# One block per layer: the second norm and the odd input projection taken into the feed-forward block, front reordered

## What is computed

```
def trunk(x, ...):
    for i in range(2):
        if i == 0: y = even_mixer(x, ...)   # latent attention and a gated short convolution -> w_o_e
        else:      y = odd_mixer(x, ...)    # x @ w_in_o, conv of 4 taps, silu, gated delta rule -> w_o_o
        x = layer_norm(ALPHA * x + y, ln_mix_g[i], ln_mix_b[i])
        h = x @ w_ff_in                     # 1024 -> 2 * 2816: gate, up
        gate = conv3(h[..., :2816])         # per channel, 3 taps
        y = (silu(gate) * up) @ w_ff_out    # 2816 -> 1024
        x = layer_norm(ALPHA * x + y, ln_ff_g[i], ln_ff_b[i])
def odd_mixer(x, ...):
    qkv, z, a, bt = split(x @ w_in_o)       # 3072, 1024, 8, 8 columns
    qkv = silu(conv4(qkv)); beta = sigmoid(bt)
    g = -exp(a_log) * softplus(a + dt_bias) # summed inside chunks of 64 tokens: G
    ...                                     # delta rule over 17 chunks and 8 heads, rms norm, * silu(z), @ w_o_o
```

## Time and profile before

| | us |
|---|---|
| runs of the kernel before | 3303.55, 3304.77, 3307.37 |
| the profiled execution, its own time | 3306.29 |
| its span, first to last instruction | 3304.5 |
| PE matmul busy | 3082.5 (93%), 22758 matmuls |
| PE weight loads busy | 2930.9 (89%) |
| DVE busy | 1582.0 (48%) |
| POOL busy | 1062.7 (32%) |
| ACT busy | 722.6 (22%) |
| mean granted clock of TensorE, as a share of 2.4 GHz | 0.966 |

### The profile page before, as it was taken

The page is one execution under the profiler, slowest core; times in us unless marked ns, Lnnn a source line. Parts: engine busy times, 40 slices in busy tenths (PEclk is TensorE's granted clock), DMA queues, the critical chain, the costliest instruction groups (busy, mean ns, idle before and its releaser), DMA issues. The chain is left out here.

```text
span 3304.5 us, 54021 instructions
## 1 busy us (share of the span) xinstructions
PE 3082.5 (93%) x22758; PEld 2930.9 (89%) x22758; DVE 1582.0 (48%) x2701; ACT 722.6 (22%) x1346; POOL 1062.7 (32%) x708
## 2 busy tenths in 40 slices
PE   7998999999999999985999949998899999999996
PEld 6997668899999999965999948887889999999994
DVE  2337574654443443453666645554364344434444
ACT  2112473210100111121121234553131001001102
POOL 2233101243233232204323246774443332232220
PEclk8999999999999999997999979998899999999998
DMA  5120102011111111103322233331401111111101
GB/s 160 44 62 7 45 1 81 13 52 45 39 42 56 44 45 39 33 1 107 99 85 86 79 80 85 82 89 40 125 21 50 50 53 39 45 41 43 39 26 55
DMA packets 261885, 184.23 MB, mean 56 GB/s; under 512 B 49775, under 2 KB 246749, under 8 KB 261541
## 3 DMA queue, kind: packets, MB, share of 16 engines
q1 hardware_dynamic: 261669, 181.09, 18.8%
HBM read 147.19 MB, written 33.84 MB: 55 GB/s over the span
## 5 line engine op out<-in xcount | busy, mean ns | idle before, releaser
L145 PE MATMUL ps<-xhi,whi 128*128 128x364 f32 (+1 forms) x3528 | 1171.1, 332 | 67.6 <-POOL wlo L138 41.9
L146 PE MATMUL ps<-xlo,whi 128*128 128x364 f32 (+1 forms) x3528 | 1166.3, 331 | 0.0
L151 PE MATMUL ps<-xhi,wlo 128*128 128x364 f32 (+1 forms) x3528 | 1165.3, 330 | 0.0
L145 PEld LDWEIGHTS ps<-xhi,whi 128*128 128x128 f32 (+1 forms) x3528 | 664.5, 188 | 75.7 <-POOL wlo L138 42.5
L146 PEld LDWEIGHTS ps<-xlo,whi 128*128 128x128 f32 (+1 forms) x3528 | 664.9, 188 | 4.9 <-issue 1.0
L151 PEld LDWEIGHTS ps<-xhi,wlo 128*128 128x128 f32 (+1 forms) x3528 | 663.9, 188 | 3.3 <-issue 0.5
L1730 DVE TENSOR_TENSOR z<-ps,z 128x364 f32<-128x364 f32 x528 | 283.3, 537 | 639.9 <-PE ps L151 639.9
L1500 POOL TENSOR_SCALAR whi<-wraw 128x1024 fp32r<-128x1024 f32 x136 | 149.7, 1101 | 1035.1 <-PE ps L151 1034.7
L1503 POOL TENSOR_TENSOR wlo<-wraw,whi 128x1024 fp32r<-128x1024 f32 x136 | 349.4, 2569 | 11.3
L145 PE MATMUL ps<-oo_hhi,whi 128*128 128x364 f32 x528 | 173.8, 329 | 0.3 <-DVE z L1730 0.3
L145 PE MATMUL ps<-eo_hhi,whi 128*128 128x364 f32 x528 | 173.8, 329 | 0.3 <-DVE z L1730 0.3
(11 more groups left out here) (406 smaller groups left out, 4343.5 us busy)
## 6 DMA issues: line engine op xcount, KB each, us to landing
wraw<-in_w_ff_in SPq DMA_DIRECT2D x88, 512.0 KB, 3.9
wraw<-in_w_ff_out SPq DMA_DIRECT2D x44, 512.0 KB, 3.6
qkvz<-oin_out SPq DMA_DIRECT2D x32, 546.0 KB, 2.8
wraw<-in_w_in_o SPq DMA_DIRECT2D x32, 512.0 KB, 4.4
z<-residual SPq DMA_DIRECT2D x6, 1456.0 KB, 8.7
wraw<-in_w_in_e SPq DMA_DIRECT2D x17, 512.0 KB, 3.9
residual<-z SPq DMA_DIRECT2D x1, 4368.0 KB, 11.8
dn_gb<-gates SPq DMA_DIRECT2D x34, 128.0 KB, 3.7
```

Source lines behind the costliest of these rows:

```text
L145: one = pe.matmul(out, whi, xhi, start=start, stop=False)
L146: two = pe.matmul(out, whi, xlo, start=False, stop=False)
L151: return pe.matmul(out, wlo, xhi, start=False, stop=stop)
```

## The change

It makes `layer_block` out of `out_ffn_block`, `layer_norm_block`, `odd_in_block` and `gates_block`; the last three are removed. The attention and delta blocks keep their computation. The pieces below stand, in order, in the streams of PE (`tail` and the loop over TAIL, then what follows it for the odd layer and for the last), DVE (the loop from 3 on), POOL (the wait ahead of the split of an odd unit) and DVE again (in the mixer).

```diff
+    TAIL = [(0, o, (NCH - 2,)) for o in range(KD)] + [(0, o, (NCH - 1,)) for o in range(KD)]
+    TAIL += [(q, o, (NCH - 2, NCH - 1)) for q in (1, 2) for o in range(KD)]
...
+            def tail(i):
+                q, o, cs = TAIL[i]
...
+                if i < SPL:
+                    pe.wait_ge(s("free0"), SPL * (FT - 1) + i + 1)
+                elif i < 2 * SPL:
+                    pe.wait_ge(s("free1"), SPL * (FT - 2) + i + 1)
+                else:
+                    pe.wait_ge(s("out_free"), DONE + i - BANKS + 1)
+                group(m.ps[:, i % BANKS, 0:NS], q, o, cs)
...
-            for part in range(4):
-                outs(NCH - 1, part)
+            for i in range(NT):
+                tail(i)
+                if i == 2 * KD:
+                    mean(3)
+                if i == 2 * KD + 4:
+                    variance(3)
+                if i == 3 * KD + 4:
+                    mean(4)
...
+            if odd:
+                odd_product(0, 0)
+                mean(5)
+                odd_product(1, 0)
+                variance(4)
+                odd_product(2, 0)
+                odd_product(3, 0)
+                odd_product(0, 1)
+                odd_product(1, 1)
+                variance(5)
+                odd_product(2, 1)
+                odd_product(3, 1)
+                for i in range(4):
+                    odd_product(i, 2)
+                for i in range(4, NODD):
+                    for q in range(SPL):
+                        odd_product(i, q)
...
+            else:
+                mean(5)
+                variance(4)
+                variance(5)
+                for n, (q, c, k0) in enumerate(ROWS):
...
+            for i in range(3, NT):
+                tail(i)
+                if i == 2 * KD:
+                    centre(3)
+                if i == 2 * KD + 2:
+                    square_sums(3)
+                if i == 2 * KD + 4:
+                    normed(3, range(0, HALF))
+                if i == 2 * KD + 5:
+                    normed(3, range(HALF, KD))
+                if i == 3 * KD + 3:
+                    centre(4)
+            square_sums(4)
+            centre(5)
+            normed(4, range(KD))
+            square_sums(5)
+            normed(5, range(KD))
...
+                    if kind == "odd" and t <= 4:
+                        pool.wait_ge(s("out_full"), DONE + NT)
+                    elif kind == "odd":
+                        g, j = odd_group(t - 4)
+                        pool.wait_ge(s(f"odd_full{g}{SPL - 1}"), j + 1)
...
-                    if q >= 1 and j == 1:
+                    if q >= 1 and j == 0:
                         centre(q - 1)
```

More of the change, by code:

```diff
@@ L1384, in out_ffn_block @@
     order += [("out", FT - 2), ("out", FT - 1)]
+    NODD = 1 + 4 * HEADS if odd else 0
+    order += [("odd", i) for i in range(NODD)]
     nth = {unit: n for n, unit in enumerate(order)}
@@ L1479, in _ @@
                     continue
-                if n >= RAW + ahead or not ahead:
+                if n >= loaded:
                     arrived[n % RAW] += 1
                     pool.wait_ge(s(f"w_raw{n % RAW}"), 16 * arrived[n % RAW])
+                if kind == "odd" and t == 0:
+                    split_gates(n)
+                    continue
                 if kind == "mix":
@@ L1509, in _ @@
                     residual(2)
+                if (kind, t) == ("odd", 3):
+                    pool.memset(raw[:, :, 0:GAP], 0.0).then_inc(s("raw0"), 1)
+                    residual(3)
+                    residual(4)
+                if (kind, t) == ("odd", 4):
+                    residual(5)
+                if (kind, t) == ("odd", 8):
+                    masks()
         @block.tensor
@@ new lines, in high, with kept @@
+            def high(r, k):
+                cols = SPLIT[r % SPL]
+                act.wait_ge(s("normed"), KD * r + k + 1)
+                b = m.par[:, bias(r) + k:bias(r) + k + 1]
+                if r < SPL or odd:
+                    act.activation(m.xhi[:, k, cols], m.z[:, k, cols], ACT.Identity, bias=b).then_inc(s("hi"), 1)
+                else:
+                    act.activation(m.z[:, k, cols], m.z[:, k, cols], ACT.Identity, bias=b).then_inc(s("biased"), 1)
+            def kept(i, q):
+                g, j = odd_group(i)
+                h, k = (i - 1) // 4, (i - 1) % 4
+                act.wait_ge(s(f"odd_full{g}{q}"), j + 1)
+                if i > 4 and q == 0:
+                    act.wait_ge(s("taps"), 12 * (h - 1) + 4 * (k + 1)) if k < 3 else act.wait_ge(s("tile3"), h)
+                src = m.ps[:, 3 * g + q, 0:NS]
+                if i == 0:
+                    src, dst = m.ps[0:AB, 3 * g + q, 0:NS], ab[:, SPLIT[q]]
+                elif k == 3:
+                    dst = gb[:, SPLIT[q]]
+                else:
+                    dst = raw[:, k, GAP + q * NS:GAP + (q + 1) * NS]
+                act.copy(dst, src).then_inc(s(f"odd_free{g}{q}"), 1)
@@ new lines, in sigmoid @@
+            def sigmoid(i):
+                h, k = (i - 1) // 4, (i - 1) % 4
+                if k < 3:
+                    act.wait_ge(s("taps"), 12 * h + 4 * (k + 1))
+                if i >= 2:
+                    act.wait_ge(s(f"tile{(k + 3) % 4}"), h + 1 if k else h)
+                if k == 3:
+                    for q in range(SPL):
+                        g, j = odd_group(i)
+                        act.wait_ge(s(f"odd_free{g}{q}"), j + 1)
+                act.activation(sg[:, :], (gb[:, 0:TW] if k == 3 else cv[:, :]), ACT.Sigmoid).then_inc(s("sig_odd"), 1)
@@ L1661, in _ @@
                 act.copy(hhi[:, c % 2, k, :], cv[:, :]).then_inc(s("h_hi"), 1)
+            act.preload_act_table_set(LN_EXP)
+            act.wait_ge(s("h_lo"), FT)
+            for c in range(HALF):
+                squares(3, c)
+            root(3)
+            for k in range(KD):
+                high(3, k)
+            for c in range(HALF):
+                squares(4, c)
+            if odd:
+                kept(0, 0)
+            root(4)
+            if odd:
+                kept(1, 0)
@@ new lines, in low, with normed @@
+            def low(r, k):
+                cols = SPLIT[r % SPL]
+                dve.wait_ge(s("hi"), KD * r + k + 1)
+                dve.scalar_tensor_tensor(m.xlo[:, k, cols], m.z[:, k, cols], m.par[:, bias(r) + k:bias(r) + k + 1],
+                                         m.xhi[:, k, cols].bitcast(F32), ALU.add, ALU.subtract).then_inc(s("lo"), 1)
+            def normed(r, ks):
+                split = r < SPL or odd
+                for k in ks:
+                    scaled(r, k)
+                    if split and k - 2 >= ks[0]:
+                        low(r, k - 2)
+                for k in ks[-2:] if split else ():
+                    low(r, k)
```

1017 lines of the change are left out of this document (474 added, 543 removed).

## The result

The changed kernel takes 3157.93 us (median of 4 runs, 3155.97 to 3160.32) where the kernel before takes 3306.07 (4 runs, 3303.55 to 3308.78): a ratio of 0.9552, 95% interval 0.9536 to 0.9569, 148 us less. The forecast was 3166, range 3143 to 3196. The profiled execution took 3156.76 us with a span of 3154.0, so the span fell by 150.5 from 3304.5.

A forecast was written before the change was run, and what follows sets the result against it. PE's matmuls were taken to bound the dense stretches, so only the bare pieces between them could be saved. The terms summed to -139 us from 3306.3, giving 3167.3, or 3166 us at the median, range 3143 to 3196.

The forecast's parts named there:

- C: Norms of both mixers: steps moved one tile earlier shorten PE's waits; -7.6 us (0 to -11).
- A: Front, first loads: x loads ahead of z stores and six x buffers start products sooner; -9 us (-3 to -15).
- D: Second norm of layer 0: mostly hidden under the out product's tail and odd products; -67 us (-45 to -74).
- E: Odd projection to delta block: gates, transposes and masks move under odd units, leaving 21 us; -19 us (-14 to -23).
- B: Key rows in the front: copies on ACT remove PE's 13.0 us wait and slow clock; -15.4 us (-12 to -16).
- G: Last norm and row stores: tail hides part, 51 us left bare; -21 us (-15 to -28).
- dense from 37 to 41: Sign for the front: PE's first dense stretch would start near 37 to 41 us.
- F: Delta to second layer: POOL's semaphore clearing bounds the start, so loading w_o_o ahead gains 0 us (0 to -5).
- Rival 1: Norms not hidden, as DVE and POOL shut each other out in the tail: 21 us late, 3188 us; chance 0.15.
- Rival 2: More goes: front reaches its bound, tail stalls don't show, second layer starts 3 us sooner; 3150 us, chance 0.10.
- Rival 3: A part fails: x loads still wait or mixers' stalls only move; A and half of C lost, 3178 us, chance 0.04.
- Rival 4: Odd projection becomes bound by DVE and ACT, 9 us above PE a unit; 3383 us, slower than before, chance 0.03.

The follow-up runs named there:

- the run of the front alone: Kernel before with only the front's new order (six x buffers, x loads ahead of z stores, a product moved ahead): 3294.46 us against 3307.33.
- the run alone: Kernel before with only the copies of the key rows moved from DVE to ACT: 3290.48 us, ratio 0.9950.
- the two experiments on A and C: Kernel before with only the front's new order, 3294.46 us; kernel before with only the mixers' norm steps one tile earlier, 3292.50 us.
- the doubled low parts: Changed kernel with POOL making each weight unit's low part twice from odd unit 5 on: 3160.30 us, ratio to the kernel before 0.9554.

## Why the forecast held, step by step

3166 against 3157.93 is closer than the parts are. C came out 7 us larger than forecast, A, D and E 2 to 3 us each and B 1; G fell 1.3 short, and the delta block, which the forecast took as unchanged, was 4.0 us longer by variation. That these four us went the other way is luck.

**A, -9 forecast, -12.0 measured.** Two things were missing. The slow clock over the product behind 46.15, 1.7 us, goes with the wait ahead of it; it stood in the bound of -15 and not in the sum, and 0.4 more went behind the key rows' wait. And the product that I had at 41 starts earlier, since the product moved ahead covers tile 8's low part whole: at 36.2 + 4.1 = 40.3 in the run of the front alone (tile 8 turned at 35.60), 0.7 sooner. In the changed kernel tile 8 is turned at 33.24, as "near 33" had it, that product, now the fourth, starts at 37.99, and the fourth product of the kernel before at 51.85: 13.9 sooner. The sign "dense from 37 to 41" missed: PE is dense from 28.2 on.

**B, -15.4 and -16.4.** Wait and clock as read from the earlier trace rows: taken from the fourth product on, the edit is worth 15.4 alone and 15.4 in the changed kernel (308.6 to 293.2 us). What was named as next (the last rope step) held nothing. The 1.0 more in the run alone is variation of the front.

**C, -7.6 and -14.6, outside its bounds of 0 to -11.** The term was the wait alone. The same clock cost that I counted in B, behind 13.0 us, stands behind a wait of 4.28 too. 2.9 and 2.7 us of clock were missing, and I kept 1.8 where 1.32 stayed; some 0.6 of the second layer's 7.5 can't be put down to either, and two profiles with that block unaltered had it 0.3 and 1.9 us shorter than the kernel before.

**D, -67 and -69.0.** The 7 us put down for DVE and POOL shutting each other out came: 4.3 of wait at the last mean, and 2.6 of clock behind it (7.1 us at 0.63). The cause was right; the size was a guess, and the clock was no part of it. The 1.2 for other stalls didn't come. Odd products of splits 1 and 2 never waited, as the count of due times had it. The wait at the mean is POOL's by the last layer's tail. But the two experiments show that taking it away, by PE's order or by POOL's, only moves it: DVE has next to no slack between 1400 and 1435.

**E, -19 and -22.3.** 9.9 us were counted from the last matmul to the end of the block, and SP's next load came at 1821.73, 9.2 us behind it; from there 8.5 to the first sum instead of 8.9. The step that was too high is "two transposes of state rows take 2": they run beside ACT and cost nothing.

**F, 0 and +0.5, right by half of the reason.** POOL's clearing bounds the start (5.72 us ahead of its first memset instead of 5.20, which is the 0.5), but only because the loads stand ahead; without them it is 3.4 more, since the change put the residual first. The forecast looked at the load that was added and not at the order of the queue.

**G, -21 and -19.7.** Behind the last group 50.4 us are left, and 51 were counted: the terms held. The other 1.7 I put down to the two means and the variance that now stand ahead of the last group: D counted them for layer 0, G didn't. The variance of split 5 waited 10.7 us for the chain of squares, and ten stores of 1.4 us each (3133.16 to 3147.06) end the kernel. One row was misread: the 15.83 us of the earlier trace rows are all nine stores together, 1.8 us for one.

**Rival 1** (norms not hidden) was right about the exclusion and wrong about its reach: 4.0 us on four sums, 3.0 on two sums of squares (4.74 against 1.74 in the last layer, where POOL rests), not 21. Its sign was met in part: two of the four sums took over 2 us and PE waited for them, but the low parts took 0.90 and held nothing. **Rival 2** (more goes): the result, 3158, lies midway between its 3150 and my 3166, but through C, A and E; of what it named, only a part of the front came. **Rival 3** falls by the two experiments on A and C. **Rival 4** falls by the doubled low parts.

## What to carry to other kernels

Price a stall in a dense stretch by what the clock does behind it, too: in this kernel's profiles 4.3 us of wait cost 6.0 to 7.2, 3.3 us cost 5.0, 2.5 us cost 4.2 and a single 1.3 us cost 1.3, but two waits of 0.9 us within 3 us of each other cost 3.5. So making a wait short can be worth more than its length, and cutting one into two may be worth nothing. Where a norm is spread under the next product, count the engine that makes it (DVE here) over the whole stretch, since neither PE's order nor delaying POOL gave anything once it was full. And when loads are put ahead, look at what is now first in the queue behind them.

## What the runs showed that I had not expected

- The final product of each odd unit (L2080) takes 2.67 us on average over 24, where it took 1.30 in the kernel before; three of the taps keep their 1.5. The product now falls just when POOL splits the next unit (POOL from 1706.15 for 2.39 us, the product from 1706.41 for 3.29). That it does so because ACT copies all banks was not tried. It costs 33 us of DVE's time, of which the first tap, now clear of POOL, gives back 16 (0.90 us instead of 1.58 over 24). The kernel loses nothing by it, since PE's unit of 12.0 us covers it.

```profile
L2071 DVE SCALAR_TENSOR_TENSOR eo_conv<-eo_raw,par,eo_conv 128x1092 f32<-128x1092 f32 x72 | 108.3, 1505 | 2.5
L2080 DVE TENSOR_TENSOR eo_ob<-eo_conv,eo_sig 128x1092 f32<-128x1092 f32 x24 | 64.1, 2671 | 73.5 <-ACT eo_sig L1789 73.5
```

- One weight load of 512 KB issued behind a residual load of 1456 KB held POOL for 3.44 us.
- Why the delta block varies by 7 us between executions of the same code was not tried and stays open; its first step (36.7 to 41.1 us) and one in the middle (14.9 to 17.3) carry most of it.
